# Masking the unseen keys of stick-breaking attention by a large negative number added in PSUM, in a one-core Trainium2 decoder step

## Chip, cores and metric

The program runs on 1 core of one Trainium2 chip. The metric is the device time of one execution in microseconds (us), as the median of several runs.

## The reference, cut to what matters

One inference step of a decoder with two layers (`DEPTH = 2`), for one prompt of 256 tokens and 8 sample tokens (264 columns in all). Every layer runs three groups of heads side by side on the output of one in-projection: an S5 state-space branch, stick-breaking attention with 4 heads of 64, and retention. An out-projection and a ConvFFN follow. Only the attention of the prompt is touched here:

```python
def stick_breaking(q, k, v, bias, q_pos, k_pos):
    z = (jnp.einsum('bqhd,bkhd->bhqk', q, k).astype(F32) * (SB_HEAD_DIM ** -0.5)
         + bias.astype(F32)[None, :, None, None])
    valid = k_pos[None, :] < q_pos[:, None]
    log_beta = jax.nn.log_sigmoid(z)
    log_rest = jnp.where(valid, log_beta - z, 0.0)
    tail = lax.cumsum(log_rest, axis=3, reverse=True) - log_rest
    w = jnp.where(valid, jnp.exp(log_beta + tail), 0.0)
    return jnp.einsum('bhqk,bkhd->bqhd', w, v.astype(F32))
```

A key that is not before its query (`valid` false) must contribute nothing twice: nothing to the running sum `tail`, and weight zero.

## The kernel before

All activations lie transposed, features on the 128 partitions and the 264 tokens along the free dimension. Weights stream through a ring of 5 buffers of 512 KB, one "unit" (128 output features) at a time. The program of each engine is written out by hand, and semaphores join them; nothing reorders it. On TensorE the in-projection of a layer is a loop over units 0 to 19 (`tile8`, L432, 16 passes of about 0.22 us each), and the small matmuls of the three branches are set between units by the table `AT`: for the attention, `ss` (sample scores), `sc` (transposes of the sample scores, L735, then the prompt's scores, `sb_scores`), `tails` and `values`. In layer 0 `sc` stands behind unit 7, in layer 1 behind unit 5. `b00` to `b11` are the input matmuls of the S5 branch (L554), `c0` and `c1` its output matmuls (L566, L571), which wait for VectorE's last product (semaphore `s5x`, rows `sfin`).

`sb_scores` calls `causal` for each of the 4 heads. The features of a head take 64 partitions: heads 0 and 2 the lower 64, heads 1 and 3 the upper 64. Keys lie on the output's partitions and queries along the free dimension, so the bank of a head holds 384 columns: keys 0 to 127 with all 256 queries (L622), and keys 128 to 255 with queries 128 to 255 (L623). The two blocks on the diagonal (columns 0 to 127 and 256 to 383) are those with unseen keys.

ScalarE brings the scores to SBUF (`sb_first`, L1145, buffer `Z`, in rows `ZT`) and makes log(1+exp(-|z|)) of them (`SPL`, the other half of `ZT`, L1148 to L1155). VectorE adds max(z, 0) in `sb_second` (L1874) and sets the unseen part of the diagonal blocks to zero with two products by a 0/1 mask (L1877, L1878). TensorE sums over keys in `sb_tails` (L744 to L751), VectorE subtracts (`sb_third`), ScalarE takes the exponential, and VectorE sets the unseen part of the weights to zero with two more products (`sb_mask`, L1894, L1895), before `sb_values` and `sb_sample_values` use the weights. Behind `sb_mask` VectorE takes up the retention (`ret_inner`, L1838), which waits for TensorE (L633).

ScalarE's program in the same place: it copies each finished unit out of PSUM (L1223), and in layer 0 it also builds the S5 tables in between, three activations per piece (L1091 to L1093). Where a step is called, ScalarE's work for it comes last in its turn.

Of the kernel before, what the change touches and what calls it, by code (L numbers as in the profile page):

```python
# [23 lines left out]
F32R = mybir.dt.float32r  # L24
ALU = mybir.AluOpType
ACT = mybir.ActivationFunctionType

P = 128
SEQ, NS = 256, 8
# [4 lines left out]
HEADS, DH, DV = 4, 64, 128  # L34
# [5 lines left out]
DEC = 384  # L40
# [53 lines left out]
PER_LAYER = _at - 2 * KT  # L94
N_VEC = 2 * KT + DEPTH * PER_LAYER

CONSTS = ["mean_v", "mean_d", "ident", "tri", "ones", "mask", "mean_w", "less_mean"]
LOG_GAMMA = np.log1p(-np.exp2(-5.0 - np.arange(HEADS)))
TWO_PI = 2.0 * math.pi
TWO_PI_HI = float(np.float32(6.28125))  # L100
# [1 line left out]
PI_SAFE = 3.1415925  # L102
TWO_PI_IN = 6.283185
ROUND = 1.5 * 2.0**23
ROUND_15 = 1.5 * 2.0**8


def hybrid_step(nc, A, O):
    with ExitStack() as ctx:
# [12 lines left out]
        def at(name, shape, over=None, dt=F32):  # L122
            size = int(np.prod(shape[1:])) * 4
            if over is None:
                place[name] = here[0]
                here[0] += -(-size // 32) * 32
            else:
                place[name] = place[over[0]] + 4 * over[1]
            return nc.alloc_sbuf_tensor_at(name, shape, dt, offset=place[name])
# [7 lines left out]
        Z, SPL = ZT[:, 0], ZT[:, 1]  # L137
# [62 lines left out]
        rms2 = at("rms2", [P, 2, T], over=("sqt", 0))  # L200
        ysb = at("ysb", [P, 2, 256], over=("sqt", 0))
        sqa = at("sqa", [P, 2, T], over=("acc", 0))
        eps_all, halfpi = at("eps_all", [P, 2]), at("halfpi", [P, 1])
        eps_t = {LN_EPS: eps_all[:, 0:1], RMS_EPS: eps_all[:, 1:2]}
        conv = at("conv", [P, CSLOTS, T], over=("yd", 0))
# [7 lines left out]
        vec = at("vec", [P, N_VEC])  # L213
        cst = at("cst", [P, len(CONSTS), P])
        dtab = at("dtab", [P, HEADS, SEQ])
# [9 lines left out]
        assert here[0] <= nc.sbuf_usable_end, (here[0], nc.sbuf_usable_end)  # L225
        C = {n: cst[:, i] for i, n in enumerate(CONSTS)}
        ps = ctx.enter_context(nc.psum_tensor("ps", [P, 8, 512], F32))
# [13 lines left out]
        def needr(eng, name, q, k):  # L241

            eng.wait_ge(S(name), sum(RAWS[:q]) + k)
# [29 lines left out]
        def need(eng, name, L, k):  # L273

            eng.wait_ge(S(name), L * PERL[name] + k)

        def in_bank(i):
# [8 lines left out]
                "rsq": 1, "otev": 1, "rot": 1, "osamp": 1, "ro": 4, "oev": 4, "gmean": 4, "gd": 4, "gsq": 4,  # L286
                "gvar": 4, "gv1": 1, "gr": 1, "gsil": 2,
                "catc": 4, "qz0": 1, "qb": 2, "sbz": 4, "zev": 4, "sbzs": 1, "zrow": 1, "zst": 1, "zs": 1,
                "spe": 1, "spl": 1, "sbs": 4, "zsub": 4, "sbss": 1, "zsubs": 1, "zmin": 1, "wexp": 1, "w": 1,
                "sby": 2, "ybev": 2, "sbys": 1, "ysev": 1, "yst": 1, "ybs": 1,  "catb": 2,  # L290
                "cat_hi": KT, "cat_lo": KT, "up_free": N_UP, "fc": N_UP, "fs": FT, "prod": FT,
                "hff_hi": FT, "hff_lo": FT, "spre": 1,
# [23 lines left out]
        def bcast(ap, shape, axis):  # L316
            return ap.unsqueeze(axis).to_broadcast(shape)
# [92 lines left out]
        def _(pe):  # L410
            E = Engine(pe, "pe_step")
            mm = nc.tensor.matmul
# [205 lines left out]
            def causal(bank, h, k0, q0):  # L618

                r = slice(64 * (h % 2), 64 * (h % 2) + 64)  # L620
                kk, qq = hb[r, k0 + h // 2], hb[r, q0 + h // 2]
                mm(bank[:, 0:SEQ], kk[:, 0:P], qq[:, 0:SEQ], start=True, stop=True)  # L622
                return mm(bank[:, SEQ:DEC], kk[:, P:SEQ], qq[:, P:SEQ], start=True, stop=True)  # L623

            def ret_inner(L):

# [82 lines left out]

            def sb_scores(L):  # L710
                needr(pe, "rawh", 2 * L, RAW)
                for h in range(HEADS):
                    need(pe, "in_evac", L, KB + 1 + h // 2 - RAW)
                    bank = claim(4 + h, "zev", L, h + 1)
                    E.did(causal(bank, h, KB, QB_), "sbz")
# [35 lines left out]
                E.did(mm(bank[:, 32:64], C["tri"], s1, start=True, stop=True), "sbss")  # L751

            def sb_values(L):
                need(pe, "w", L, 1)
                need(pe, "vbt", L, 1)
                for ht in range(2):
                    bank = claim(6 + ht, "ybev", L, ht + 1)
                    for h in (2 * ht, 2 * ht + 1):
                        r = 64 * (h % 2)
                        o = bank[r:r + 64]  # L760
                        w0, w1 = Z[:, h * DEC:h * DEC + SEQ], Z[:, h * DEC + SEQ:(h + 1) * DEC]
                        mm(o[:, 0:SEQ], VBt[:, 0, 64 * h:64 * h + 64], w0, start=True, stop=False,
                           tile_position=(0, r))
                        ins = mm(o[:, P:SEQ], VBt[:, 1, 64 * h:64 * h + 64], w1, start=False, stop=True,
                                 tile_position=(0, r))
                    E.did(ins, "sby")

            def sb_sample_values(L):

                need(pe, "w", L, 1)  # L770
                pe.wait_ge(S("ld_kv"), 16 * NS * PAGES * (2 * L + 2))
                bank = claim(3, "ysev", L, 1)
                for bl in range(2):
                    for pg in range(PAGES):
                        for g in range(4):
                            b = 2 * g + bl
                            wc = 4 * DEC + 32 * pg + 4 * b
                            ins = mm(bank[32 * g:32 * g + HEADS, 256 * bl:256 * bl + 256], Z[:, wc:wc + HEADS],  # L778
                                     kv[:, b, pg], start=(pg == 0), stop=(pg == 1), tile_position=(0, 32 * g))
                E.did(ins, "sbys")  # L780
# [170 lines left out]
        def _(act):  # L951
            E = Engine(act, "act_step")
            f = nc.scalar.activation
# [262 lines left out]
            for L in range(DEPTH):  # L1216
                at_ = AT[L]
                ln_in(L)
                for i in range(RAW, N_IN):
# [24 lines left out]
                    if i == at_["ss"]:  # L1244
# [2 lines left out]
                            act.wait_ge(S("ld_vec"), 32)  # L1247
                        E.did(f(zsb[:], ps[:, 2, 0:2 * P], ACT.Identity, scale=DH ** -0.5, bias=pv(L, "biasr")), "zrow")
                    if i == at_["sc"]:
                        need(act, "zst", L, 1)  # L1250
                        E.did(nc.scalar.copy(Z[:, 4 * DEC:4 * DEC + 64].rearrange("p (k r) -> p k r", r=8),
                                             sample_rows(3, 2 * P)[:, :, 0:8]), "zs")
                        sb_first(L)
# [152 lines left out]
        def _(dve):  # L1406
            E = Engine(dve, "dve_step")
            tt, ts, stt = nc.vector.tensor_tensor, nc.vector.tensor_scalar, nc.vector.scalar_tensor_tensor
# [195 lines left out]
            dt, ldr, t4, n, r, sn, cs, ab, den, t0, t1, t2, t3 = (disc[:, i] for i in range(13))  # L1604
# [257 lines left out]
                E.settle()  # L1862
                E.did(tt(spre[:], spre[:], c10, ALU.add), "spre")

            def diagonals(buf):
                v = buf[:, 0:4 * DEC].rearrange("p (h c) -> p h c", h=HEADS)
                return v[:, :, 0:P], v[:, :, SEQ:DEC]

            mask = bcast(C["mask"], [P, HEADS, P], 1)

            def sb_second(L):

                need(dve, "spe", L, 1)
                E.did(stt(SPL[:], Z[:], 0.0, SPL[:], ALU.max, ALU.add))  # L1874
                E.settle()
                d0, d1 = diagonals(SPL)
                E.did(tt(d0, d0, mask, ALU.mult))  # L1877
                E.did(tt(d1, d1, mask, ALU.mult), "spl")  # L1878

            def sb_third(L):  # L1880

# [5 lines left out]
                E.did(tt(Z[:, 4 * DEC:4 * DEC + 64], Z[:, 4 * DEC:4 * DEC + 64], ps[:, 3, 0:64], ALU.subtract), "zsubs")  # L1887
                E.settle()
                E.did(ts(Z[:], Z[:], 0.0, None, ALU.min), "zmin")

            def sb_mask(L):
                need(dve, "wexp", L, 1)
                d0, d1 = diagonals(Z)
                E.did(tt(d0, d0, mask, ALU.mult))  # L1894
                E.did(tt(d1, d1, mask, ALU.mult), "w")  # L1895

            def sb_out(L):
                for ht in range(2):
# [100 lines left out]
            for L in range(DEPTH):  # L1999
# [25 lines left out]
                sb_third(L)  # L2025
                s5_skip(L, 1)
                rotary(L)
                sb_mask(L)
                if EARLY[L]:
                    lower_early(L, 0)  # L2030
                ret_inner(L)
# [77 lines left out]
                for i in range(N_UP):  # L2109
                    need(dve, "fc", L, i + 1)  # L2110
                    bank, c = hraw[:, i] if i < RAW_UP else ps[:, i % UP_BANKS], conv[:, i % CSLOTS]
# [89 lines left out]
def constants():  # L2201

    f = np.float32
    eye = np.eye(P, dtype=f)
    k, q = np.arange(P)[:, None], np.arange(P)[None, :]
    cst = np.stack([np.full((P, P), 1 / P, f), np.full((P, P), 1 / D_MODEL, f), eye, (k >= q).astype(f),
                    np.ones((P, P), f), (k < q).astype(f), np.full((P, P), 1 / 256, f),
                    np.full((P, P), -1 / D_MODEL, f)], 1)
    pos = np.concatenate([np.arange(SEQ), np.full(NS, SEQ)]).astype(f)
    inv = (10000.0 ** (-np.arange(32, dtype=f) / 32)).astype(f)[np.arange(P) % 32]  # L2210
    ang = (inv[:, None] * pos[None, :]).astype(f)
    rope = np.stack([np.cos(ang), np.sin(ang)], 1).astype(f)
    gap = np.arange(SEQ)[None, None, :] - np.arange(P)[:, None, None]
    dtab = np.where(gap >= 0, np.exp(LOG_GAMMA[None, :, None] * np.maximum(gap, 0)), 0.0) * DH ** -0.5
    left = SEQ - 1 - (np.arange(P)[:, None] + P * np.arange(2)[None, :])
    kdec = np.exp(LOG_GAMMA[None, None, :] * left[:, :, None])
    gam = np.exp(LOG_GAMMA)[np.arange(P) // 32][:, None]
    steps = np.broadcast_to(np.arange(SEQ, dtype=f), (P, SEQ))
    return {"cst": cst, "rope": rope, "dtab": dtab.astype(f), "kdec": kdec.astype(f), "gam": gam.astype(f),
            "steps": steps}  # L2220
# [91 lines left out]
```

## Time and profile before

| | |
|---|---|
| time, median of 3 runs | 674.18 us (674.04 to 674.87) |
| the profiled execution's own time | 674.94 us |
| its span (first to last instruction) | 673.1 us |
| TensorE busy | 661.4 us, 98% |
| TensorE weight loads busy | 613.4 us |
| VectorE busy | 569.1 us, 85% |
| ScalarE busy | 415.2 us, 62% |
| GpSimd busy | 91.2 us, 14% |

Busy time is the time in which an engine has at least one instruction under way; matmuls overlap each other, so their modelled durations (0.39 us for one 264-column pass) are longer than the distance between their starts (0.22 us), and it is the starts that tell the pace. An fp32 matmul shows as two passes. Positions are microseconds from the start of the span.

### The profile page before, as it was taken

To read this page: it belongs to the slowest core of one execution; us is meant where nothing else is said; L and a number is where in the kernel's file an instruction comes from. 1 tells how busy PE (TensorE), PEld (TensorE's weight loads), DVE (VectorE), ACT (ScalarE), POOL (GpSimd) and SP (SyncE) were. 2 spreads that over 40 slices of the span, in tenths; PEclk is the share of its full clock that TensorE was granted. 3 is DMA by queue.
4 is the path that set the end of the run, shared out by engine and by line. 5 is a ranking of instruction groups with operands and counts; after the bars stand their busy time and mean duration, and the time that the engine had idled before them with its cause. 6 is when DMAs were issued, how large, how long until landed. Compare 5 with 4: busy or idle time off the path is not lost. (4 is left out here: it accounts for less than half of the span.)

```text
span 673.1 us, 13390 instructions
## 1 busy us (share of the span) xinstructions
PE 661.4 (98%) x5024; PEld 613.4 (91%) x5024; DVE 569.1 (85%) x1195; ACT 415.2 (62%) x690; POOL 91.2 (14%) x90
## 2 busy tenths in 40 slices
PE   8999999999999999999999999999999999999997
PEld 6777887989999999999987787989999999999996
DVE  5999999989998988789588998898999898884653
ACT  5776348758676666655847536786867666663343
POOL 0000010150222222200200000106012222220001
PEclk9999999999999999999999999999999999999999
DMA  8777540746674655664456463354765556555411
GB/s 315 244 274 220 188 130 6 274 112 227 203 255 151 201 187 184 197 192 142 142 179 228 167 206 125 115 200 167 199 211 197 188 170 193 176 196 190 161 57 66
DMA packets 42915, 121.82 MB, mean 181 GB/s; under 512 B 5538, under 2 KB 15170, under 8 KB 42338
## 3 DMA queue, kind: packets, MB, share of 16 engines
q1 hardware_dynamic: 40466, 115.22, 51.7%
q0 software_dynamic: 1088, 4.11, 2.5%
q10 hardware_dynamic: 1296, 1.63, 0.8%
q8 instruction: 40, 0.66, 0.4%
q14 instruction: 25, 0.20, 0.1%
HBM read 115.33 MB, written 5.61 MB: 180 GB/s over the span
## 5 line engine op out<-in xcount | busy, mean ns | idle before, releaser
L1579 DVE TENSOR_TENSOR w_lo<-ring,w_hi 128x1024 fp32r<-128x1024 f32 x144 | 175.4, 1220 | 30.6 <-ACT w_hi L964 29.0
L439 PE MATMUL ps<-x_hi,w_hi 128*128 128x264 f32 x672 | 191.0, 284 | 1.0 <-DVE x_lo L1529 1.0
L440 PE MATMUL ps<-x_lo,w_hi 128*128 128x264 f32 x672 | 190.4, 283 | 0.0
L441 PE MATMUL ps<-x_hi,w_lo 128*128 128x264 f32 x672 | 190.3, 283 | 0.0
L964 ACT CAST w_hi<-ring 128x1024 fp32r<-128x1024 f32 x144 | 150.2, 1043 | 59.4 <-PE ps L441 58.7
L439 PEld LDWEIGHTS ps<-x_hi,w_hi 128*128 128x128 f32 x672 | 126.5, 188 | 1.9 <-issue 1.8
L440 PEld LDWEIGHTS ps<-x_lo,w_hi 128*128 128x128 f32 x672 | 126.6, 188 | 0.0
L441 PEld LDWEIGHTS ps<-x_hi,w_lo 128*128 128x128 f32 x672 | 126.0, 188 | 0.0
L432 PE MATMUL ps<-x,ring 128*128 128x264 f32 x480 | 112.1, 390 | 0.1
L432 PEld LDWEIGHTS ps<-x,ring 128*128 128x128 f32 x480 | 89.1, 190 | 18.9 <-issue 2.2
L439 PE MATMUL ps<-hff_hi,w_hi 128*128 128x264 f32 x352 | 100.0, 284 | 0.0
L441 PE MATMUL ps<-hff_hi,w_lo 128*128 128x264 f32 x352 | 99.9, 284 | 0.0
L440 PE MATMUL ps<-hff_lo,w_hi 128*128 128x264 f32 x352 | 99.9, 284 | 0.0
L2190 POOL TENSOR_TENSOR hff_lo<-conv,hff_hi 128x264 fp32r<-128x264 f32 x44 | 52.7, 1198 | 213.8 <-ACT hff_hi L1208 213.8
L441 PEld LDWEIGHTS ps<-hff_hi,w_lo 128*128 128x128 f32 x352 | 66.3, 188 | 0.0
L439 PEld LDWEIGHTS ps<-hff_hi,w_hi 128*128 128x128 f32 x352 | 66.1, 188 | 0.0
L440 PEld LDWEIGHTS ps<-hff_lo,w_hi 128*128 128x128 f32 x352 | 66.1, 188 | 0.0
L1365 ACT ACTIVATE conv<-ps,vec 128x264 f32<-128x264 f32 x84 | 47.8, 569 | 22.2 <-PE ps L441 22.1
L1208 ACT CAST hff_hi<-conv 128x264 fp32r<-128x264 f32 x44 | 18.2, 414 | 48.8 <-DVE conv L1600 48.8
L2117 DVE SCALAR_TENSOR_TENSOR conv<-ps,vec,conv 128x254 f32<-128x254 f32 x84 | 40.5, 482 | 3.0
L1223 ACT COPY hb<-ps 128x264 f32<-128x264 f32 x34 | 12.7, 374 | 46.0 <-PE ps L432 43.5
L503 PE MATMUL ps<-zg,ring 128*128 128x266 f32 x160 | 39.0, 388 | 1.6 <-DMA ring<-in_units 1.6
(364 smaller groups left out, 1091.0 us busy)
## 6 DMA issues: line engine op xcount, KB each, us to landing
ring<-in_units SPq DMA_DIRECT2D x187, 512.0 KB, 3.5
kv<-in_kpool SPq DMA_DIRECT2D x32, 128.0 KB, 2.4
kv<-in_vpool SPq DMA_DIRECT2D x32, 128.0 KB, 2.4
SR<-in_sret SPq DMA_DIRECT2D x2, 1024.0 KB, 5.9
out_rsample<-SR POOLq DMA_DIRECT2D x2, 1024.0 KB, 5.1
out_kv<-hb ACTq DMA_DIRECT2D x2, 528.0 KB, 4.4
VBC<-v_rows POOLq DMA_DIRECT2D x8, 128.0 KB, 3.5
out_y<-x SPq DMA_DIRECT2D x3, 264.0 KB, 2.1
```

The source lines that it names most:

```text
L432: ins = mm(out, ring[:, ring_slot(n), k], rhs(k), start=(k == 0), stop=(k == 7))
L439: mm(out, wh, hi, start=start, stop=False)
L440: mm(out, wh, lo, start=False, stop=False)
L441: return mm(out, wl, hi, start=False, stop=stop)
L503: ins = mm(out[:, 0:GB], ring[:, ring_slot(raw_unit(q, i)), k], zgs[q % 2][:, k], start=(k == 0), stop=(k == KT - 1))
L964: E.did(nc.scalar.copy(w_hi[:, split_slot(i)], ring[:, ring_slot(n)]), "w_hi")
L1208: E.did(nc.scalar.copy(hff_hi[:, p], conv[:, (2 * p + 1) % CSLOTS]), "hff_hi")
L1223: E.did(nc.scalar.copy(hb[:, i], ps[:, in_bank(i), 0:T]), "in_evac")
L1365: E.did(f(conv[:, i % CSLOTS], source, ACT.Identity, scale=pv(L, "cw2", i), bias=pv(L, "cb", i)), "fc")
L1579: E.did(tt(w_lo[:, slot], ring[:, ring_slot(L * UNITS + i)], w_hi[:, slot].bitcast(F32), ALU.subtract), "w_lo")
L2117: E.did(stt(c[:, 2:SEQ], bank[:, 0:SEQ - 2], pv(L, "cw0", i), c[:, 2:SEQ], ALU.mult, ALU.add), "up_free")
L2190: E.did(tt(hff_lo[:, p], conv[:, (2 * p + 1) % CSLOTS], hff_hi[:, p].bitcast(F32), ALU.subtract), "hff_lo")
```

## The change

The constant `mask` (1 where the key is seen) becomes `unseen` (0 where it is seen, -2^30 where it is not). ScalarE makes fp32r copies of it and of the identity matrix, in layer 0 only. `causal` adds a third matmul to each head: identity times `unseen`, once for each of the two diagonal blocks (256 columns in one instruction, fp32r, all 128 partitions), accumulated onto the scores. The four mask products of each layer on VectorE go, with the semaphore `w`; `sb_values` waits for the exponential instead.

```diff
-CONSTS = ["mean_v", "mean_d", "ident", "tri", "ones", "mask", "mean_w", "less_mean"]
+CONSTS = ["mean_v", "mean_d", "ident", "tri", "ones", "unseen", "mean_w", "less_mean"]
+UNSEEN = -2.0**30
...
+        ident_r = at("ident_r", [P, P], dt=F32R)
+        unseen_r = at("unseen_r", [P, P], dt=F32R)
...
-                mm(bank[:, 0:SEQ], kk[:, 0:P], qq[:, 0:SEQ], start=True, stop=True)
-                return mm(bank[:, SEQ:DEC], kk[:, P:SEQ], qq[:, P:SEQ], start=True, stop=True)
+                mm(bank[:, 0:SEQ], kk[:, 0:P], qq[:, 0:SEQ], start=True, stop=False)
+                mm(bank[:, SEQ:DEC], kk[:, P:SEQ], qq[:, P:SEQ], start=False, stop=False)
+                diagonal = bank.rearrange("p (a c) -> p a c", a=2)[:, :, 0:P]
+                return mm(diagonal, ident_r[:], bcast(unseen_r[:], [P, 2, P], 1), start=False, stop=True)
...
                 needr(pe, "rawh", 2 * L, RAW)
+                pe.wait_ge(S("unseen"), 2)
...
-                need(pe, "w", L, 1)
+                need(pe, "wexp", L, 1)
...
                     if i == at_["sc"]:
+                        if L == 0:
+                            act.wait_ge(S("ld_cst"), 16)
+                            E.did(nc.scalar.copy(ident_r[:], C["ident"]), "unseen")
+                            E.did(nc.scalar.copy(unseen_r[:], C["unseen"]), "unseen")
                         need(act, "zst", L, 1)
...
-                E.did(stt(SPL[:], Z[:], 0.0, SPL[:], ALU.max, ALU.add))
-                E.settle()
-                d0, d1 = diagonals(SPL)
-                E.did(tt(d0, d0, mask, ALU.mult))
-                E.did(tt(d1, d1, mask, ALU.mult), "spl")
+                E.did(stt(SPL[:], Z[:], 0.0, SPL[:], ALU.max, ALU.add), "spl")
...
-            def sb_mask(L):
-                need(dve, "wexp", L, 1)
-                d0, d1 = diagonals(Z)
-                E.did(tt(d0, d0, mask, ALU.mult))
-                E.did(tt(d1, d1, mask, ALU.mult), "w")
...
                 rotary(L)
-                sb_mask(L)
```

TensorE at `sc` of layer 0, from the transposes of the sample scores (L735) over the four heads to the next unit of the in-projection; before:

```order
L735 MATMUL ps<-cst,zsb 128x128
L622 MATMUL ps<-hb 128x256 [waits buev,in_evac,rawh]
L623 MATMUL ps<-hb 128x128
L622 MATMUL ps<-hb 128x256 [waits buev,in_evac]
L623 MATMUL ps<-hb 128x128
L432 MATMUL ps<-x,ring 128x264 [waits ld_w3,in_evac]
```

and of the changed kernel, the same place up to the second head (its line numbers are 3 to 6 higher; its first head also waits for the two copies, semaphore `unseen`):

```order
L741 MATMUL ps<-cst,zsb 128x128
L625 MATMUL ps<-hb 128x256 [waits in_evac,buev,unseen,rawh]
L626 MATMUL ps<-hb 128x128
L628 MATMUL ps<-unseen_r,ident_r 128x2x128
L625 MATMUL ps<-hb 128x256 [waits buev,in_evac]
L626 MATMUL ps<-hb 128x128
L628 MATMUL ps<-unseen_r,ident_r 128x2x128
```

Each head's two matmuls on 64 partitions are now followed by one on 128.

ScalarE at `sc` of layer 0: the copy of unit 7, the last piece of the S5 table, and the step's own work; before:

```order
55 L1223 COPY hb<-ps 128x264
56 L1091 ACTIVATE tab_84<-steps,fhi 128x256
57 L1092 ACTIVATE tab_84<-steps,rnd,fhi 128x256
58 L1093 ACTIVATE low<-steps,flo 128x256
59 L1251 COPY ZT<-ps 128x64
60 L1145 ACTIVATE ZT<-ps,vec 128x384 x4
```

and of the changed kernel:

```order
55 L1229 COPY hb<-ps 128x264
56 L1097 ACTIVATE tab_84<-steps,fhi 128x256
57 L1098 ACTIVATE tab_84<-steps,rnd,fhi 128x256
58 L1099 ACTIVATE low<-steps,flo 128x256
59 L1258 CAST ident_r<-cst 128x128
60 L1259 CAST unseen_r<-cst 128x128
61 L1261 COPY ZT<-ps 128x64
62 L1151 ACTIVATE ZT<-ps,vec 128x384 x4
```

The two copies stand behind the table's three activations and ahead of what ScalarE did first at `sc`.

## Rows read from the trace of the kernel before

**Rows 1.** The page: busy time, and the clock granted in 40 slices
```profile
PE 661.4 (98%) x5024; PEld 613.4 (91%) x5024; DVE 569.1 (85%) x1195; ACT 415.2 (62%) x690; POOL 91.2 (14%) x90
PEclk9999999999999999999999999999999999999999
```

**Rows 2.** Waits of TensorE: for whom, total us, times, longest us
```profile
PE ps L503 <- DMA ring<-in_units: 1.6, 1, 1.6
PE ps L566 <- DVE sfin L1790: 1.2, 2, 0.7
```

**Rows 3.** Chain that ended last, layer 1: start us, us, what
```profile
390.52 1.75 DVE ZT L1874
392.29 0.69 DVE ZT L1877
392.98 0.61 DVE ZT L1878
```

**Rows 4.** Timeline of VectorE, layer 1: start, us, instructions, idle before and releaser
```profile
409.35 0.69 DVE L1894 TENSOR_TENSOR ZT<-ZT,cst 128x512 f32<-128x512 f32 x1
...
412.79 0.42 DVE L1838 TENSOR_TENSOR RI<-ps,dtab 128x256 f32<-128x256 f32 x1 [0.99 <-PE ps L633]
```

**Rows 5.** Timeline of TensorE in several short windows, `sc` of layer 0
```profile
44.72 0.38 PE L735 MATMUL ps<-cst,zsb 128*128 128x128 f32 x2
44.83 0.27 PE L735 MATMUL ps<-cst,zsb 128*128 128x128 f32 x1
45.03 0.49 PE L622 MATMUL ps<-hb 64*128 64x256 f32 x2
45.35 0.39 PE L622 MATMUL ps<-hb 64*128 64x256 f32 x2
45.56 0.28 PE L623 MATMUL ps<-hb 64*128 64x128 f32 x2
46.22 0.49 PE L623 MATMUL ps<-hb 64*128 64x128 f32 x4
46.64 0.71 PE L432 MATMUL ps<-x,ring 128*128 128x264 f32 x2
46.97 0.61 PE L432 MATMUL ps<-x,ring 128*128 128x264 f32 x2
```

**Rows 6.** Timeline of TensorE, fp32r matmuls of 264 columns
```profile
438.30 0.28 PE L452 MATMUL ps<-xe_lo,we_hi 128*128 128x264 f32 x1
438.42 0.28 PE L453 MATMUL ps<-xe_hi,ring_lo 128*128 128x264 f32 x1
```

**Rows 7.** Timeline of ScalarE, `sc` of layer 0
```profile
44.92 0.38 ACT L1223 COPY hb<-ps 128x264 f32<-128x264 f32 x1 [2.30 <-PE ps L432]
45.19 0.51 ACT L1091 ACTIVATE tab<-steps,fhi 128x256 f32<-128x256 f32 x1
...
46.49 0.20 ACT L1251 COPY ZT<-ps 128x64 f32<-128x64 f32 x1
46.59 2.00 ACT L1145 ACTIVATE ZT<-ps,vec 128x384 f32<-128x384 f32 x4
```

**Rows 8.** Timeline of TensorE, layer 0, units 9 to 11 and what follows
```profile
54.40 0.73 PE L554 MATMUL ps<-hb,s5b 32*128 32x264 f32 x8
55.05 7.39 PE L432 MATMUL ps<-x,ring 128*128 128x264 f32 x32
62.72 0.73 PE L554 MATMUL ps<-hb,s5b 32*128 32x264 f32 x8 [0.28 <-ACT work L1139]
64.17 1.07 PE L566 MATMUL ps<-work,cf 128*32 128x256 f32 x16 [0.73 <-DVE sfin L1790]
```

**Rows 9.** Timeline of TensorE, layer 1, scores and `c1`
```profile
365.69 0.71 PE L622 MATMUL ps<-hb 64*128 64x256 f32 x4
...
366.98 0.78 PE L622 MATMUL ps<-hb 64*128 64x256 f32 x4 [0.36 <-ACT hb L1223]
...
367.91 0.49 PE L432 MATMUL ps<-x,ring 128*128 128x264 f32 x1
...
400.07 0.39 PE L751 MATMUL ps<-ZT,cst 128*128 128x32 f32 x2
400.98 0.43 PE L566 MATMUL ps<-work,cf 128*32 128x256 f32 x4 [0.52 <-DVE sfin L1790]
```

More of the change, by code:

```diff
@@ L288, in hybrid_step @@
                 "catc": 4, "qz0": 1, "qb": 2, "sbz": 4, "zev": 4, "sbzs": 1, "zrow": 1, "zst": 1, "zs": 1,
-                "spe": 1, "spl": 1, "sbs": 4, "zsub": 4, "sbss": 1, "zsubs": 1, "zmin": 1, "wexp": 1, "w": 1,
+                "spe": 1, "spl": 1, "sbs": 4, "zsub": 4, "sbss": 1, "zsubs": 1, "zmin": 1, "wexp": 1,
                 "sby": 2, "ybev": 2, "sbys": 1, "ysev": 1, "yst": 1, "ybs": 1,  "catb": 2,
@@ L768, in sb_sample_values @@
             def sb_sample_values(L):
-                need(pe, "w", L, 1)
+                need(pe, "wexp", L, 1)
                 pe.wait_ge(S("ld_kv"), 16 * NS * PAGES * (2 * L + 2))
@@ L1863, in conv_prev @@
                 E.did(tt(spre[:], spre[:], c10, ALU.add), "spre")
[L1865 to L1869, printed above, removed]
             def sb_second(L):
                 need(dve, "spe", L, 1)
-                E.did(stt(SPL[:], Z[:], 0.0, SPL[:], ALU.max, ALU.add))
-                E.settle()
-                d0, d1 = diagonals(SPL)
-                E.did(tt(d0, d0, mask, ALU.mult))
-                E.did(tt(d1, d1, mask, ALU.mult), "spl")
+                E.did(stt(SPL[:], Z[:], 0.0, SPL[:], ALU.max, ALU.add), "spl")
             def sb_third(L):
@@ L2206, in constants @@
     cst = np.stack([np.full((P, P), 1 / P, f), np.full((P, P), 1 / D_MODEL, f), eye, (k >= q).astype(f),
-                    np.ones((P, P), f), (k < q).astype(f), np.full((P, P), 1 / 256, f),
+                    np.ones((P, P), f), np.where(k < q, 0, UNSEEN).astype(f), np.full((P, P), 1 / 256, f),
                     np.full((P, P), -1 / D_MODEL, f)], 1)
```

## The prediction

> **What bounds the kernel now.** I read the busy times first: TensorE is busy for 661.4 of 673.1 us and VectorE for 569.1 [rows 1]. TensorE is in fact never without work for long: the list of its waits has 1.6 us once, near the start, for a weight unit, and nothing longer [rows 2]. So the time is TensorE's queue plus its few waits, and whatever another engine saves counts only where TensorE waited for it. The chain that ended last can mislead here. In layer 1 it runs through the very products that are removed, 0.69 and 0.61 us [rows 3], but only because TensorE at 400.98 waited for VectorE's `sfin` (0.52 us); the chain follows that wait back, while TensorE streamed units without a stop all the way. The price of VectorE's lateness is that wait, not the length of the products. In the same places I looked at what VectorE does behind `sb_mask`: it waits 0.99 us for TensorE [rows 4], in layer 1; it is as long in layer 0. Time saved there only lengthens VectorE's own wait.
>
> **What goes.** Two products per place, 0.69 + 0.61 us from start to start [rows 3, 4], four places: 5.2 us of VectorE. Those of `sb_mask` lie ahead of VectorE's wait for TensorE and are worth nothing. Those of `sb_second` make `sfin` of hf 1 ready 1.3 us earlier. In layer 1 that removes TensorE's wait ahead of L566: the last pass of L751 starts at 400.07 + 0.11, runs 0.11, a change of array shape costs 0.09 (below), so L566 could start at 400.39 and started at 400.98 [rows 9]: 0.59 us, the most that the whole saving can give. In layer 0 nothing waited there.
>
> **What the eight mask matmuls cost.** The trace has no fp32r matmul of 256 columns; fp32r matmuls of 264 columns follow each other every 0.12 us [rows 6]. Alone that would be 4 x 0.12 = 0.48 us per layer. But look at what stands around them [rows 5]. A head's scores are matmuls on 64 of the 128 array rows, and heads 0 and 1 (and 2 and 3) lie on different halves: their passes start in pairs, two L622 at 45.03, two at 45.35, two L623 at 45.56. All four heads take 45.03 to 46.64, 1.61 us, where one head by itself would need 0.32 + 0.21 + 0.11 + 0.11 = 0.75. A matmul on 128 partitions behind each head ends that pairing. And passing from one shape to the other is itself slow: L735 (128 rows) has a pace of 0.11 (44.72, 44.83), but L622 (64 rows) follows after 0.20, and its own first pass takes 0.32 where the next takes 0.21: 0.09 of gap and 0.11 of weight load that nothing covers. The way back is the same: the last L623 pass (a pass is drawn 0.27 long) starts at 46.22 + 0.49 - 0.27 = 46.44, L432 at 46.64, its second pass at 46.97 where the pace is 0.22. The changed program passes from 64 to 128 rows and back in every head. Per head: 0.32 + 0.21 + 0.11 + 0.11 + 0.09 = 0.84 for the scores and the gap, then 0.11 + 0.12 + 0.09 = 0.32 for the mask matmul and the gap: 1.16 us. Four heads are 4.64, less 0.09 because unit work follows the last mask in the same shape, and less 0.11 of its first weight load: 4.44 in place of 1.61, **+2.83 us per layer**.
>
> The Trainium skill says the same in TensorEngine Tiling (Tiling Modes, Key Properties): changing the tiling mode, and not just the tile, drains the engine, and tiles in one mode run independently. The rows just read agree, with 0.20 us for a change. Without that rule one would price the masks at 0.48 us a layer.
>
> The bounds: not below 0.12 per mask (no drain, pairs kept: +0.48 a layer), since fp32r has no faster row; not above the two passes of an fp32 matmul of 256 columns, 2 x 0.21 = 0.43, with both changes of shape (+4.1 a layer). I take 0.12 with the changes, because the new instruction is nearest in kind to L452 and the neighbours are exactly those of rows 5.
>
> **What the wait for the copies costs, layer 0.** The order shows the two copies behind the S5 table's three activations. ScalarE comes free for its own `sc` work at 46.49 [rows 7], where L1251 starts now. A copy of 264 columns lets the next instruction start after 0.27, one of 64 after 0.10, so one of 128 after about 0.15 and done after 0.26: the second copy ends at 46.49 + 0.15 + 0.26 = 46.90, and TensorE picks it up some 0.05 later. TensorE now starts L622 at 45.03: a new wait of **1.9 us**, queued behind it all four heads and every unit after. Bounds: 1.4 (copies for nothing) to 2.2 (0.27 each and two 0.1 hand-overs). In layer 1 the copies are long done.
>
> **What absorbs it.** Layer 0 is late by 1.9 + 2.83 = 4.75 us behind the scores. TensorE then meets two waits which VectorE's S5 work sets, and that work does not hang on the scores: L432 ends its 32 passes at 62.44 and L554 starts at 62.72; with no wait it would start 0.07 before that modelled end, as it does at 54.40, so 0.35. From L554 to the next group takes 0.65 where nothing waits (54.40 to 55.05) and 1.45 here: 0.80 [rows 8]. Together 1.15 us of the delay is swallowed; **+3.6 us** goes on. I followed ScalarE and VectorE through it: ScalarE's table for hf 1 moves by some 2.3 us, into its idle time ahead of L1139; its second L1139 comes some 1.2 us late and holds VectorE by as much, which the removed products of `sb_second` give back before the tails. Later in the layer VectorE and ScalarE wait for TensorE again, so the delay stays.
>
> Layer 1: TensorE waits at 366.98 for ScalarE's copy of unit 5, halfway through the heads, so part of the new work lies in that wait: with 1.16 per head the four end at 365.69 + 4.64 - 0.09 = 370.24 instead of 367.91, +2.33, less 0.11 of the covered load: +2.2. Then the 0.59 at L566 goes (VectorE itself gets some 0.65 late, because S5's PSUM copies come later, and 1.3 early by the removed products: ready ahead of TensorE): **+1.6 us**.
>
> Sum: 3.6 + 1.6 = +5.2 us on the profiled execution's 674.94, so 680.2. That execution lay 0.76 above the median of 674.18; for the median I say **679.4 us**, +0.8%.
>
> **Rivals.**
> (a) *Masks break the pairs but change of shape is cheap.* A head is then 0.65 + 0.12 = 0.77, four 3.08: +1.47 against now. Layer 0: 1.9 + 1.5 - 1.15 = 2.3, layer 1: about +0.9 - 0.6 = 0.3. Sum +2.6, 676.8. Against it: both gaps in rows 5. Chance 0.12.
> (b) *The masks stream at 0.12 and nothing else is lost.* Layer 0: 1.9 + 0.48 - 1.15 = 1.25; layer 1: two masks exposed, 0.24 - 0.59 = -0.35. Sum +0.9, 675.1, no measurable change. Chance 0.06.
> (c) *VectorE's 5.2 us reach the end.* If VectorE sets the pace of both attention stretches, as its place in the chain suggests [rows 3], each layer gains its 2.6 and pays what (b) pays: -5.2 + 0.9 + 0.59 = -3.7, 670.5. It decides if TensorE's waits for VectorE behind the products exceed the masks' price. For it: VectorE is busy 85%. Against it: TensorE never waited over 0.7 us there [rows 2], and the 0.99 us of rows 4 have the opposite sign. Chance 0.04.
> (d) *The masks run as two passes*, 0.43 each: +0.31 x 8 = 2.5 more, 681.9. Against: fp32r rows everywhere are single. Chance 0.09.
> (e) *TensorE's clock falls in the new wait.* The clock granted is full in all 40 slices [rows 1], in spite of an idle 1.6 us [rows 2] near the start. If it fell to its lower level for the heads and one unit of layer 0, the 4.4 + 3.6 us there would take twice as long: up to +8, nothing left to hide it, 687. Chance 0.04.
> The Trainium skill's TensorE: Matmul & The Clock Gate (Part 1) says that the clock goes to 1.2 GHz when the engine has been idle; no run here shows that yet for a pause of 1.9 us.
>
> **How the numbers follow.** The forecast itself has 0.65: 679.4, by its own bounds 678.3 to 680.6. The range 676.4 to 682.0 takes in (a) and (d) and leaves out (b), (c) and (e). A measurement of this kernel tells about 0.2% (1.35 us) from no change: slower by more 0.89, same 0.07, faster 0.04.
>
> **What the changed profile would show.** In layer 0 a wait of TensorE at L625 for ScalarE's cast L1259 of about 1.9 us; L625 to the next unit 4.5 us instead of 1.61, with no two heads starting together; 0.2 us from L626's last pass to L628; the waits at L554 (62.7) and at c0 gone. In layer 1 the wait for `sfin` gone, the heads 4.5 us long. VectorE 5 us less busy, its wait ahead of the retention longer. It is wrong if L628 stands 0.12 from its neighbours, if the copies were placed where TensorE does not reach them first, or if some later wait swallows the delay.

## The result and the profile after

| | median us | runs, lowest to highest | of before, 95% interval |
|---|---|---|---|
| before | 674.3 | 4, 674.04 to 674.87 | |
| changed | 683.64 | 4, 682.87 to 685.92 | 1.0143 [1.0116, 1.017] |

The change makes the kernel 9.3 us slower, where +5.2 was forecast. The time lies above the range's end of 682.0. It also spreads over 3 us, where that of before spreads over 0.8, and it goes with TensorE's mean granted clock: 682.87 and 682.91 us at 0.995, 684.38 at 0.992, 685.92 at 0.988. The four runs of before beside it list none; in the 66 runs of before beside the experiments the mean was never under 0.998.

The page of the changed kernel's profiled execution (682.87 us, span 681.1), to be held against [rows 1]:

```profile
span 681.1 us, 13402 instructions
PE 669.4 (98%) x5032; PEld 619.1 (91%) x5032; DVE 564.5 (83%) x1187; ACT 416.5 (61%) x692; POOL 91.8 (13%) x90
PEclk9998999999999999999999999999999999999999
```

VectorE is 4.6 us less busy, near the 5.2 forecast, and TensorE 8.0 us more, with eight matmuls more. The clock row has an 8 in its fourth slice, where [rows 1] have nines only. It stands at 51 to 68 us, where the heads of layer 0 end.

TensorE's list of waits, against [rows 2] (for whom, total us, times, longest):

```profile
PE ps L625 <- issue: 2.0, 1, 2.0
...
PE ps L506 <- DMA ring<-in_units: 1.0, 1, 1.0
```

Both waits for `sfin` are gone, and one of 2.0 us has come at the first head. The timeline of TensorE at `sc` of layer 0 (start us, duration, instruction, idle before it), against [rows 5]:

```profile
44.18 0.38 PE L741 MATMUL ps<-cst,zsb 128*128 128x128 f32 x2
46.54 0.67 PE L625 MATMUL ps<-hb 64*128 64x256 f32 x2 [1.98 <-issue]
...
47.67 0.70 PE L625 MATMUL ps<-hb 64*128 64x256 f32 x2
48.20 0.38 PE L626 MATMUL ps<-hb 64*128 64x128 f32 x2
48.52 0.39 PE L628 MATMUL ps<-unseen_r,ident_r 128*128 128x256 f32 x1
48.83 0.90 PE L625 MATMUL ps<-hb 64*128 64x256 f32 x2
49.52 0.63 PE L626 MATMUL ps<-hb 64*128 64x128 f32 x2
50.09 0.58 PE L628 MATMUL ps<-unseen_r,ident_r 128*128 128x256 f32 x1
50.59 1.22 PE L625 MATMUL ps<-hb 64*128 64x256 f32 x2
51.61 0.63 PE L626 MATMUL ps<-hb 64*128 64x128 f32 x2
52.17 0.58 PE L628 MATMUL ps<-unseen_r,ident_r 128*128 128x256 f32 x1
```

No two heads start together any more. The second head takes 47.67 to 48.83, 1.16 us, the forecast's figure exactly. From 48.83 on the same instructions are slower: L628 is drawn 0.58 us long where it was 0.39, and the last head's first group 1.22 where it was 0.70. The windows show why (us, then busy time of PE, PEld, DVE, ACT and POOL, the granted clock, DMA share, GB/s):

```profile
44.00:49.00 5.00, 3.02 (x15) 2.12 (x14) 4.96 (x14) 2.81 (x9) 0.00 (x0) 1.00 0.84 330
49.00:56.00 7.00, 7.00 (x18) 5.26 (x19) 6.62 (x13) 3.22 (x4) 0.00 (x0) 0.51 0.01 2
56.00:63.00 7.00, 7.00 (x39) 5.46 (x38) 6.93 (x7) 4.43 (x7) 0.00 (x0) 1.00 0.53 175
```

TensorE ran at its lower level, half of full speed, for 6.83 us (49.20 to 56.03 in the trace), over most of the third head, the last head and most of the unit behind them. At full clock that work would have taken half as long: 3.4 us lost. 682.87 less 3.4 is 679.5.

Layer 1 in this execution ran at full clock throughout, which makes it the clean reading of the masks (to be held against [rows 9]):

```profile
371.98 0.70 PE L625 MATMUL ps<-hb 64*128 64x256 f32 x2
...
373.14 0.70 PE L625 MATMUL ps<-hb 64*128 64x256 f32 x2
...
376.31 0.39 PE L628 MATMUL ps<-unseen_r,ident_r 128*128 128x256 f32 x1
376.53 1.72 PE L435 MATMUL ps<-x,ring 128*128 128x264 f32 x7
```

The heads take 371.98 to 376.53, 4.55 us, again 1.16 each less 0.09. The unit behind them is drawn 3.72 us long in a trace where it ran at full clock (layer 0 of "early", in the experiments), where before it was 3.83: that is the 0.11 us of weight load that the forecast took off to come to its 4.44. And VectorE in that layer, against [rows 4]:

```profile
420.71 0.42 DVE L1848 TENSOR_TENSOR RI<-ps,dtab 128x256 f32<-128x256 f32 x1 [3.78 <-PE ps L638]
```

VectorE's wait for TensorE is 3.78 us where 0.99 stood. The two products that went ahead of it make 1.30 of that; the rest is that TensorE has fallen further behind than VectorE by then.

### The profile page after: what moved, and what is told of

The parts are those of the page before. It is cut to its first block, busy times and chain, and to the rows that moved or that the text cites. A ratio compares the mean times of both kernels' runs of the same rounds, so it can differ in the third digit from the quotient of the medians.

```text
span 681.1 us, 13402 instructions
## 1 busy us (share of the span) xinstructions
PE 669.4 (98%) x5032; PEld 619.1 (91%) x5032; DVE 564.5 (83%) x1187; ACT 416.5 (61%) x692; POOL 91.8 (13%) x90
## 4 chain that ended last, share of the span: by engine, by line
PE 90%; DVE 6%; issue 1%; ACT 1%; DMA 1%; SPq 0%; DVEq 0%; ACTq 0%
PE ps L442 20%; PE ps L443 20%; PE ps L444 20%; PE ps L435 16%; PE ps L506 2%; DVE z L1493 1%; DVE z L1501 1%; PE ps L625 1%; DMA ring<-in_units 1%; PE ps L557 1%; PE ps L569 1%; PE ps L732 1%; PE ps L750 1%; PE ps L704 1%; PE ps L531 1%
## 5 line engine op out<-in xcount | busy, mean ns | idle before, releaser
L435 PE MATMUL ps<-x,ring 128*128 128x264 f32 x480 | 113.5, 394 | 0.1
L435 PEld LDWEIGHTS ps<-x,ring 128*128 128x128 f32 x480 | 90.5, 193 | 19.1 <-issue 2.2
L2107 DVE SCALAR_TENSOR_TENSOR conv<-ps,vec,conv 128x255 f32<-128x255 f32 x84 | 39.8, 474 | 0.3 <-issue 0.2
```

Of the source, the lines that this page charges most:

```text
L435: ins = mm(out, ring[:, ring_slot(n), k], rhs(k), start=(k == 0), stop=(k == 7))
L2107: E.did(stt(c[:, 1:SEQ], bank[:, 0:SEQ - 1], pv(L, "cw1", i), c[:, 1:SEQ], ALU.mult, ALU.add))
```

## The experiments

My theory after the result: the forecast's sum holds at full clock, and what was missing is the clock falling, in rival (e)'s way. Two causes were open: the new wait of 2 us, or the heads themselves, which no longer run in pairs. All times are medians; "before" ran on the same chip each time. A table of the runs comes first, the reasoning after it. The clock columns are the mean granted clock of the lowest and of the highest run.

That mean has to be read with care, because it covers the whole span. In eight of the thirteen traces the last 0.4 to 2.6 us of the span are at the lower level too, while no engine computes any more and only the output is on its way out ("changed again": the last matmul ends at 678.1, the clock is at half from 680.2 to the end at 682.8). This takes up to 1.3 us off span x mean clock and costs no time. So a mean of 0.998 by itself is no sign of a fall in the work: the profiled executions of "unpaired", "no products", "layer 0" and "layer 1" have 0.998 or 0.999 and no fall before their ends. A mean of 0.997 takes some 3.4 us at the lower level or more, longer than any end in a trace.

| kernel | median us (runs) | of before, 95% | lowest run, clock | highest run, clock |
|---|---|---|---|---|
| early | 678.46 (6) | 1.0063 [1.0045, 1.0081] | 677.0, 1.000 | 681.04, 0.995 |
| wait only | 675.43 (11) | 1.0025 [1.0016, 1.0035] | 674.91, 1.000 | 677.44, 0.997 |
| grouped | 674.31 (11) | 0.9997 [0.9989, 1.0006] | 673.7, 0.999 | 674.63, 0.999 |
| filled | 682.86 (6) | 1.0113 [1.0096, 1.013] | 679.77, 0.998 | 683.4, 0.995 |
| unpaired | 674.45 (11) | 1.0002 [0.9993, 1.0011] | 674.31, 1.000 | 674.98, 0.998 |
| no products | 673.63 (11) | 0.9987 [0.9978, 0.9996] | 673.34, 1.000 | 673.79, 1.000 |
| pairs | 673.82 (11) | 0.9993 [0.9984, 1.0002] | 673.46, 1.000 | 674.87, 0.999 |
| grouped late | 674.29 (11) | 0.9997 [0.9988, 1.0007] | 673.92, 1.000 | 674.76, 0.999 |
| layer 0 | 677.44 (5) | 1.0046 [1.0032, 1.006] | 676.6, 1.000 | 679.45, 0.993 |
| layer 1 | 676.32 (6) | 1.0032 [1.002, 1.0044] | 675.96, 1.000 | 678.12, 0.997 |
| changed again | 683.78 (4) | 1.013 [1.0114, 1.0145] | 682.93, 0.994 | 684.55, 0.991 |

**Early: the changed kernel without the wait.** ScalarE's copies move into the step ahead, behind the sample scores, where TensorE still has other work.

```diff
                         E.did(f(zsb[:], ps[:, 2, 0:2 * P], ACT.Identity, ...), "zrow")
-                    if i == at_["sc"]:
                         if L == 0:
...
                             E.did(nc.scalar.copy(unseen_r[:], C["unseen"]), "unseen")
+                    if i == at_["sc"]:
```

> The changed kernel, with ScalarE's two copies made one unit earlier (behind the sample scores, where it idles). Theory A (the new wait of 2 us for the copies brings TensorE's clock down, the drained heads cost 2.83 us a layer): no wait, full clock in all slices, L0 late by 2.83 - 1.15 = 1.7, L1 by 1.6, together +3.3 on before: 677.6. Rival B (the unpaired, drained heads alone bring the clock down): a stretch at 0.5 clock remains behind the scores, 680 to 682. Rival C (the excess over the forecast is not the clock but late transfers): 681, full clock.

The wait was gone, and layer 0 ran its heads in 4.57 us at full clock. Three of six runs lost nothing to the clock: 677.0, 677.46 and 677.65, +2.7 to +3.3, which is the forecast's sum without the wait (2.83 - 1.15 in layer 0, 1.6 in layer 1: +3.3). The other three took 679.27 to 681.04, at 0.995 to 0.997. The profiled one (679.27) shows where, in windows of layer 1:

```profile
360.00:370.00 10.00, 9.87 (x69) 7.16 (x67) 9.86 (x19) 6.63 (x10) 0.00 (x0) 1.00 0.77 276
370.00:375.00 5.00, 5.00 (x17) 3.92 (x16) 4.93 (x7) 2.70 (x3) 0.00 (x0) 0.66 0.00 0
```

and in its timeline the last head:

```profile
370.05 0.39 PE L628 MATMUL ps<-unseen_r,ident_r 128*128 128x256 f32 x1
370.36 0.75 PE L625 MATMUL ps<-hb 64*128 64x256 f32 x2
370.91 0.63 PE L626 MATMUL ps<-hb 64*128 64x128 f32 x2
371.47 0.58 PE L628 MATMUL ps<-unseen_r,ident_r 128*128 128x256 f32 x1
```

TensorE had worked without a wait for 9.87 of the 10 us before, and the clock still fell to half for 3.41 us, behind three heads. So the wait isn't needed. The stretch cost 1.7 us, and 679.27 less 1.7 is 677.6, as in the undisturbed runs.

**Wait only: the kernel before with the copies and the wait, and nothing else of the change.**

```diff
                 needr(pe, "rawh", 2 * L, RAW)
+                pe.wait_ge(S("w"), 2)
...
+                        if L == 0:
+                            act.wait_ge(S("ld_cst"), 16)
+                            E.did(nc.scalar.copy(ident_r[:], C["ident"]), "w")
+                            E.did(nc.scalar.copy(unseen_r[:], C["mask"]), "w")
```

(`w` counts two more with the copies, and those who wait for it later count along.)

> The kernel before, with the two copies and TensorE's wait for them at the scores of layer 0, and nothing else: no mask matmuls, VectorE's products kept. Theory A: a wait of 1.9 us; if the wait alone brings the clock down, a stretch at 0.5 clock and 1.9 - 1.15 + 2 to 4 = +3 to +5, 677 to 679. Rival B (it takes the drained heads too): full clock and +0.8, 675.1.

The wait is there, and the heads pair again behind it:

```profile
46.52 0.79 PE L624 MATMUL ps<-hb 64*128 64x256 f32 x4 [1.98 <-issue]
```

Seven of eleven runs took 674.9 to 675.7, +0.6 to +1.4, at a mean clock of 0.998 or more: 1.9 less the 1.15 that later waits swallow. The other four took 676.95 to 677.44, all at 0.997, where none of the 66 runs of before is under 0.998. So the wait by itself brings the clock down in some runs, some 2 us each time, and explains neither every run of the changed kernel nor the size. The profiled execution is one of the seven, so no trace shows where in these four the clock fell.

**Filled: the changed kernel with four matmuls of 264 columns issued inside the wait**, so that TensorE waits for the copies without being idle.

```diff
-                pe.wait_ge(S("unseen"), 2)
...
+                    if L == 0 and h == 0:
+                        for _ in range(4):
+                            mm(bank[:, 0:T], C["tri"], x[:, 0], start=True, stop=True)
+                        pe.wait_ge(S("unseen"), 2)
```

> The changed kernel with four matmuls of 264 columns (1.8 us, results overwritten) issued on TensorE where it waits for the copies, nothing else changed. Theory A: the same lateness of the heads, but full clock: the forecast's own 679.4 (+5.2). Rival B: the clock falls as in the changed kernel, 683 to 686.

This theory fell. The median is 682.86, as slow as the changed kernel. The wait is filled and layer 0 keeps its clock, but the profiled run (682.91) loses it in layer 1, in the same place as the early kernel and for longer:

```profile
44.00:51.00 7.00, 6.85 (x32) 5.11 (x31) 6.79 (x18) 3.91 (x10) 0.00 (x0) 1.00 0.68 258
365.00:370.00 5.00, 5.00 (x24) 3.99 (x23) 4.97 (x8) 4.97 (x8) 0.00 (x0) 1.00 0.66 245
372.00:379.00 7.00, 7.00 (x18) 5.41 (x18) 6.93 (x7) 2.70 (x3) 0.00 (x0) 0.52 0.01 2
```

From 365.00 on TensorE is drawn busy for 7.00 of 7.00 us at full clock, and at 372.24 the clock falls, behind three heads again. The kernel's lowest run, 679.77 at 0.998, is the forecast's 679.4 with hardly any loss. One run is not explained by its clock alone: 682.81 at 0.997 lost 2.4 us to it at most, which leaves 680.4 or more.

**Layer 0 and layer 1: the mask behind each head in one layer only.** In the other layer the four mask matmuls stand together behind the four heads, and the copies are early in both.

```diff
...
-                    E.did(causal(bank, h, KB, QB_), "sbz")
+                    ins = causal(bank, h, KB, QB_, L == 0)
+                    if L == 0:
+                        E.did(ins, "sbz")
+                if L != 0:
+                    for h in range(HEADS):
+                        diagonal = ps[:, 4 + h].rearrange("p (a c) -> p a c", a=2)[:, :, 0:P]
+                        E.did(mm(diagonal, ident_r[:], bcast(unseen_r[:], [P, 2, P], 1), start=False, stop=True), "sbz")
```

> Early copies; a mask matmul behind each head in layer 0, all four behind the heads in layer 1. At full clock: layer 0 +2.83 - 1.15 = +1.7, layer 1 -0.1: 675.9 to 676.0. If the drained heads bring the clock down by themselves, part of the runs has a mean clock of 0.997 or less and lies 1.5 to 3.5 us higher, and the profile may show the stretch behind the scores of layer 0.

> The mirror image: a mask matmul behind each head in layer 1 only. At full clock: layer 0 swallows 0.48 us, layer 1 +2.2 - 0.6 = +1.6: 675.9. The two of them should add up to what the changed kernel with early copies showed in its undisturbed runs (677.0 to 677.65). Part of the runs longer with a lower clock, as in the other.

With a mean clock of 0.998 or more they took 676.6 and 677.27 ("layer 0", +1.9 and +2.6) and 675.96 to 676.56 ("layer 1", +1.3 to +1.9). The lowest of each add up to +3.2, which is what the early kernel shows at full clock. The 677.27 is the profiled execution; its trace has a wait of 1.21 us at 362.17, ahead of layer 1's sample scores, which the change does not touch; the trace of before has no such wait. Each has runs with the clock down as well: 677.44 to 679.45 at 0.993 to 0.997 (three of five) for layer 0, 677.43 and 678.12 at 0.997 (two of six) for layer 1. So separated heads in either layer are enough for runs with a lower clock. Neither profiled execution has such a fall, so for layer 0 without the wait no trace shows the place.

**Grouped, grouped late and pairs: all the masks, but fewer changes of array shape.** Grouped has them behind all four heads in both layers; grouped late is the same with the copies where the change has them; pairs has two masks behind each two heads. Grouped:

```diff
-                    E.did(causal(bank, h, KB, QB_), "sbz")
+                    causal(bank, h, KB, QB_)
+                pe.wait_ge(S("unseen"), 2)
+                for h in range(HEADS):
+                    diagonal = ps[:, 4 + h].rearrange("p (a c) -> p a c", a=2)[:, :, 0:P]
+                    E.did(mm(diagonal, ident_r[:], bcast(unseen_r[:], [P, 2, P], 1), start=False, stop=True), "sbz")
```

> Early copies, and the four mask matmuls behind all four heads instead of one behind each: the pairs stay, one change of shape as before. If the price of the mask matmuls is the change of shape and the lost pairing: masks cost 0.48 us a layer; L0 swallows it in its waits (0), L1 +0.5 - 0.59 = -0.1: 674.2, full clock. Rival (each mask matmul is dear by itself, 0.43 or more): +1.7 a layer, 675.5 to 677.

> The four masks behind all four heads, the copies where the changed kernel has them: the heads (1.6 us) cover ScalarE's way to the copies, TensorE waits only some 0.3 us ahead of the first mask, and layer 0 swallows it: 674.2, as with early copies. If the wait were the dear part of the change wherever it stands, +1.5 or more.

and pairs:

```diff
-                    E.did(causal(bank, h, KB, QB_), "sbz")
+                    causal(bank, h, KB, QB_)
+                    for g in ((h - 1, h) if h % 2 else ()):
+                        diagonal = ps[:, 4 + g].rearrange("p (a c) -> p a c", a=2)[:, :, 0:P]
+                        E.did(mm(diagonal, ident_r[:], bcast(unseen_r[:], [P, 2, P], 1), start=False, stop=True), "sbz")
```

> Early copies, two mask matmuls behind each pair of heads (0 and 1, 2 and 3): pairs kept, one more return trip between shapes than with all four masks at the end, 2 x 0.2 us a layer. Layer 0: +0.48 + 0.4, swallowed; layer 1: 365.69 + 0.75 + 0.2 + 0.24 + 0.2 = 367.1, no wait for the copy of unit 5, end at 368.4 against 367.91 less 0.1: +0.4, less 0.6: 674.1. Full clock if it takes longer stretches without pairs.

None of their 33 runs has a mean clock under 0.998, and none of the three kernels can be told from the kernel before. The timeline of grouped, layer 0:

```profile
44.00 0.71 PE L625 MATMUL ps<-hb 64*128 64x256 f32 x4
...
45.61 0.73 PE L722 MATMUL ps<-unseen_r,ident_r 128*128 128x256 f32 x4
46.18 2.16 PE L435 MATMUL ps<-x,ring 128*128 128x264 f32 x9
```

The heads keep their 1.61 us, and the four masks cost 45.61 to 46.18, 0.57 us in place of 2.94 (4.55 less 1.61). The wait of grouped late shrinks to what the pairs leave of it, because the heads no longer wait for the copies:

```profile
46.16 0.74 PE L722 MATMUL ps<-unseen_r,ident_r 128*128 128x256 f32 x4 [0.32 <-ACT unseen_r L1260]
```

And pairs, layer 0, 2.49 us from the first head to the unit:

```profile
44.72 0.71 PE L625 MATMUL ps<-hb 64*128 64x256 f32 x4
...
45.58 0.50 PE L722 MATMUL ps<-unseen_r,ident_r 128*128 128x256 f32 x2
46.01 0.71 PE L625 MATMUL ps<-hb 64*128 64x256 f32 x4
...
46.87 0.51 PE L722 MATMUL ps<-unseen_r,ident_r 128*128 128x256 f32 x2
47.21 1.05 PE L435 MATMUL ps<-x,ring 128*128 128x264 f32 x4
```

**Unpaired: the kernel before with its heads in the order 0, 2, 1, 3**, so that the first and the last run alone on their half of the array, with no mask between.

```diff
-                for h in range(HEADS):
+                for n, h in enumerate((0, 2, 1, 3)):
                     need(pe, "in_evac", L, KB + 1 + h // 2 - RAW)
-                    bank = claim(4 + h, "zev", L, h + 1)
+                    bank = claim(4 + h, "zev", L, n + 1)
```

ScalarE takes the scores in the same order.

> The kernel before with the heads in the order 0, 2, 1, 3 (same arithmetic), so that neighbours lie on the same 64 array rows; no mask matmuls, no added change of shape. If lost pairing alone costs: heads 2.5 us instead of 1.6, about +1.0 a layer; L0 swallows it, L1 +1.0: 675.3. For the clock: if half the array and sparse work suffice to bring it down, some runs show a mean clock under 0.998 and are 2 to 4 us longer; if it takes the drains, none does.

Layer 0's heads went from 1.61 us to 2.26 (44.83 to 47.09), layer 1's from 2.22 to 2.88. The time did not move, where I expected about a microsecond: layer 1's heads are 0.66 us longer, and the wait for `sfin` in [rows 9], which swallows up to 0.59 us of a delay ahead of it, is gone from the trace. I had counted that wait for the change and overlooked it here. All eleven runs have a mean clock of 0.998 or more. Heads 2 and 1 still pair in the middle, so this loses half of the pairing, not all of it.

**No products: the kernel before without its four VectorE products** per layer's attention (two in `sb_second`, two in `sb_mask`), so that nothing masks the unseen keys.

```diff
-                need(pe, "w", L, 1)
+                need(pe, "wexp", L, 1)
...
-                E.did(stt(SPL[:], Z[:], 0.0, SPL[:], ALU.max, ALU.add))
-                E.settle()
-                d0, d1 = diagonals(SPL)
-                E.did(tt(d0, d0, mask, ALU.mult))
-                E.did(tt(d1, d1, mask, ALU.mult), "spl")
+                E.did(stt(SPL[:], Z[:], 0.0, SPL[:], ALU.max, ALU.add), "spl")
...
                 rotary(L)
-                sb_mask(L)
```

> The kernel before without VectorE's four mask products (unseen keys are not masked at all). What the saving is worth by itself: TensorE's wait for sfin in layer 1 goes, -0.6 us: 673.7. Rival (VectorE sets the pace): -2.6 to -5.2, 669 to 671.7.

It gained 0.75 us, with TensorE's wait for `sfin` in layer 1 gone. That is all that 5.2 us of VectorE time are worth here, and so about the most that the change could have gained with masks that cost TensorE nothing.

**Changed again**, with no edit, to have more runs of it:

> The changed kernel once more, for the spread of its runs. If the forecast's sum was right at full clock and all the rest is clock, a run's time less the time its clock lost (span x (1 - mean clock)) is 679 to 680 in every run, and its lowest run is not under 679.

All four runs are under 0.995. The profiled one has two stretches, of 6.83 us in layer 0 and of 3.41 us (376.42 to 379.83) in layer 1:

```profile
48.00:56.00 8.00, 8.00 (x24) 6.00 (x23) 7.58 (x19) 3.60 (x5) 0.00 (x0) 0.57 0.03 10
372.00:381.00 9.00, 9.00 (x34) 6.90 (x35) 8.86 (x17) 4.97 (x8) 0.00 (x0) 0.81 0.19 64
```

Taking from each time its span x (1 - mean clock): 682.93 less 4.1 is 678.8, and 684.55 less 6.1 is 678.4. With the clock's last digit 0.34 us is uncertain each way. I had written that this would not come under 679; it does by half a microsecond. But the 6.1 counts too much: the two stretches in which TensorE worked at half clock, 6.83 and 3.41 us, cost 5.1 us, and the rest comes from the 2.6 us at the span's end, after the last matmul. 684.55 less 5.1 is 679.4. The changed kernel's first profiled execution came to 679.5 in the same way.

## Why the prediction was right and wrong

**The bound, right.** TensorE's queue sets the time. VectorE's saving was priced at 0.59 us by its wait, and is worth 0.75 ("no products").

**The price of the masks, right.** 1.16 us per head was forecast and is measured, and 4.55 us from the first head to the unit behind the last (4.57 in layer 0 of "early"); the forecast's 4.44 is this less the unit's 0.11 of weight load, which went as well. The 0.20 us for a change of shape stands in every head: L626's second pass starts at 48.20 + 0.38 - 0.27 = 48.31, L628 at 48.52. The Trainium skill's rule in TensorEngine Tiling (Tiling Modes, Key Properties) says that changing the mode drains the engine; these rows agree, with a gap of 0.09 us in every head.

**The wait for the copies, right:** 1.98 us for 1.9. The copies follow each other after 0.19 us and last 0.28:

```profile
45.95 0.28 ACT L1258 CAST ident_r<-cst 128x128 fp32r<-128x128 f32 x1
46.14 0.29 ACT L1259 CAST unseen_r<-cst 128x128 fp32r<-128x128 f32 x1
```

**What absorbs it, right as far as it can be read at full clock:** "wait only" keeps 0.6 to 1.4 of its 1.98 us (0.75 forecast), "layer 0" costs 1.9 to 2.6 (1.7 forecast), "layer 1" 1.3 to 1.9 (1.6 forecast). With the cost of the low stretches in their traces taken out, the changed kernel's two profiled executions stand at 679.5 and 679.4; the forecast was 679.4. For the other six only the mean clock is on record, which counts the span's end too: by it all eight stand at 677.7 to 679.5, and up to 1.3 us higher if their ends ran as in "changed again".

**What failed is that the sum has no term for the clock: it takes the full clock throughout, and rival (e), "TensorE's clock falls in the new wait", got a chance of 0.04.** The clock did fall, in all eight runs of the changed kernel: every mean clock is 0.995 or lower. The step failed in three ways. Its condition was too narrow: I tied the fall to the wait. In layer 0 of the changed kernel it does come behind the wait, though not in it (2.7 us after its end in one trace, 2.2 in the other), but "early" and "filled" show it in layer 1 with no wait in front, behind the separated heads. Its size was wrong: it was priced as 8 us over a stretch that I had chosen; the stretches measured are 6.83 or 3.41 us and cost half of that, 3.4 or 1.7 us, one or two of them in the executions that have a trace: 3.4 us in the lowest run, and at most 8.2 in the highest, by its mean clock (684.1 x 0.012). And the evidence that I used against it, a full clock in spite of 1.6 us of idle near the start [rows 1, 2], was about a single pause; I never asked what the clock would do with eight changes of shape and small matmuls in 4.5 us. +5.2 for the work and some +4 for the clock make the +9.3.

The Trainium skill says in TensorE: Matmul & The Clock Gate (Part 1) that the clock follows how busy the engine has lately been, with two states, full and half. The traces agree with the two states: the clock stands at 1.00 or at its half in every stretch, and windows between them hold some of each. "Wait only" fits the first part, with 1.98 us of idle and a lower clock in four runs of eleven. "Filled" does not show it in what the profile draws as busy: 7.00 of 7.00 us ahead of the fall.

**What stays open.** Between the grouped forms, with no mean clock under 0.998 in 33 runs, and the separated heads, which lost it in three of six runs of "early", several things differ at once: the number of changes of shape, the gaps of 0.09 us, heads that fill only half of the array at a time, and the length of the whole stretch (4.55 us against 2.2 to 2.5). No experiment separates them. Why "filled" lost its clock in more runs than "early" (five of six against three of six), though TensorE was idle in neither, is open too; the number of runs, six each, is small. Nor can the runs say which runs will lose it.

A version that beats the kernel before by a measurable amount was not found. Pairs is nearest, 0.9993 [0.9984, 1.0002]: it takes 5.2 us off VectorE and gives TensorE 8 masks, and the 0.56 us by which its median is lower lie within the interval.

## What to carry to other kernels

Keep TensorE's matmuls of one array shape together: an addition over all 128 partitions belongs behind the whole group of 64-partition matmuls, not behind each (0.57 us against 2.94 per layer here). Price work taken off another engine by the wait that it ends on the bounding engine, never by its own length (5.2 us of VectorE were worth 0.75). And where an edit thins TensorE's work out for a few microseconds, by a wait or by many small gaps, count the clock as a second price, in time and in spread, and read the mean granted clock of every run before judging, and in the trace where the low stretches lie: one at the end of the span, behind the last matmul, cost nothing here.

## What the runs showed of the hardware

The granted clock fell although TensorE was drawn busy for all 7.00 us from 365.00 to 372.00 and the fall came at 372.24 ("filled", layer 1): the busy share of the profile does not show what the clock follows. In the four traces with a fall while TensorE worked, each fall lasted 3.41 or 6.83 us, and the matmuls inside it took about twice their time. With a 2 us wait ("wait only") the mean clock was down in four runs of eleven and not in seven, in one and the same program, so that one profiled execution can miss it. The mean can also mislead the other way: in eight of thirteen traces up to 2.6 us at the span's end ran at the lower level with nothing left to compute.
